# Root before the split of weight tile 1 at a branch's end, with that tile's low part on GpSimd, in a two-layer hybrid decoder step

## The reference

```python
xp = ffn_half_step(xp, g[0], g[1], ffn1_gate[l], ffn1_up[l], ffn1_down[l])
m_p, s_p = mix_prompt(rms_norm(xp, g[2]), lw)          # four head groups, input projection w_in, output w_out
xp = xp + rms_norm(m_p, g[3])
xp = ffn_half_step(xp, g[4], g[5], ffn2_gate[l], ffn2_up[l], ffn2_down[l])

def ffn_half_step(x, g_pre, g_post, w_gate, w_up, w_down):
    return x + 0.5 * rms_norm(swiglu(rms_norm(x, g_pre), w_gate, w_up, w_down), g_post)

def rms_norm(x, g):
    y = xf * lax.rsqrt(jnp.mean(xf * xf, axis=-1, keepdims=True) + NORM_EPS)
    return (y * g.astype(jnp.float32)).astype(x.dtype)
```

## Time and profile before

| | |
|---|---|
| median of 3 runs | 1602.6 us (1593.21, 1602.6, 1604.79) |
| the profiled execution's own time | 1603.99 us |
| its span in the profile | 1602.2 us |
| TensorE matmuls busy | 84% of the span |
| VectorE, ScalarE, GpSimd busy | 59%, 41%, 14% |
| mean granted TensorE clock | 0.87 of full |

### The profile page before, as it was taken

The page is one execution under the profiler, slowest core; times in us unless marked ns, Lnnn a source line. Parts: engine busy times, 40 slices in busy tenths (PEclk is TensorE's granted clock), DMA queues, the critical chain, the costliest instruction groups (busy, mean ns, idle before and its releaser), DMA issues.

```text
span 1602.2 us, 27946 instructions
## 1 busy us (share of the span) xinstructions
PE 1353.2 (84%) x9968; PEld 1257.8 (79%) x9968; DVE 944.8 (59%) x1508; ACT 652.6 (41%) x1054; POOL 216.7 (14%) x176
## 2 busy tenths in 40 slices
PE   6999979977587579999889999697866857699997
PEld 5999979966375369999889999697754735699996
DVE  4766355485654666664467654655756554666634
ACT  4655343343200255554456544434330004455543
POOL 1000010022332230000110000200323322200000
PEclk9999989967686589999989999899556966899998
DMA  6555554354461334555646556363444613255553
GB/s 213 183 184 160 163 177 131 96 155 138 147 192 49 93 105 134 184 172 162 182 129 190 172 155 181 106 199 97 129 130 138 185 38 106 83 184 183 159 168 94
DMA packets 286118, 234.15 MB, mean 146 GB/s; under 512 B 19898, under 2 KB 282018, under 8 KB 286056
## 3 DMA queue, kind: packets, MB, share of 16 engines
q1 hardware_dynamic: 286056, 233.37, 47.9%
HBM read 228.65 MB, written 5.37 MB: 146 GB/s over the span
## 4 chain that ended last, share of the span: by engine, by line
PE 76%; DVE 15%; ACT 3%; issue 3%; DMA 1%; SPq 0%; DVEq 0%; POOLq 0%; ACTq 0%
PE ps L1391 20%; PE ps L1392 19%; PE ps L1393 19%; PE ps L1590 2%; PE ps L1688 2%; DVE s L1114 2%; PE ps L1535 2%; DVE nlo L937 2%; PE ps L1687 1%; DVE yt L920 1%; PE ps L1538 1%; ACT whi L591 1%; PE ps L1504 1%; PE ps L1678 1%; PE ps L1733 1%
## 5 line engine op out<-in xcount | busy, mean ns | idle before, releaser
L1391 PE MATMUL ps<-nhi,whi 128*128 128x264 f32 x1936 | 564.2, 291 | 67.4 <-DVE nlo L937 47.0
L888 DVE TENSOR_TENSOR wlo<-raw,whi 128x1024 fp32r<-128x1024 f32 (+2 forms) x376 | 394.7, 1091 | 280.1 <-ACT whi L591 279.8
L1392 PE MATMUL ps<-nlo,whi 128*128 128x264 f32 x1936 | 558.5, 289 | 0.0
L1393 PE MATMUL ps<-nhi,wlo 128*128 128x264 f32 x1936 | 557.7, 288 | 0.0
L1391 PEld LDWEIGHTS ps<-nhi,whi 128*128 128x128 f32 x1936 | 375.2, 194 | 74.2 <-DVE nlo L937 35.9
L591 ACT ACTIVATE whi<-raw 128x1024 fp32r<-128x1024 f32 (+2 forms) x376 | 336.8, 945 | 190.9 <-PE ps L1393 113.4
L1392 PEld LDWEIGHTS ps<-nlo,whi 128*128 128x128 f32 x1936 | 375.4, 194 | 0.2
L1393 PEld LDWEIGHTS ps<-nhi,wlo 128*128 128x128 f32 x1936 | 373.2, 193 | 0.0
L1391 PE MATMUL ps<-hhi,whi 128*128 128x264 f32 x704 | 202.3, 287 | 9.1 <-DVE hlo L905 9.1
L1393 PE MATMUL ps<-hhi,wlo 128*128 128x264 f32 x704 | 201.4, 286 | 0.0
L1392 PE MATMUL ps<-hlo,whi 128*128 128x264 f32 x704 | 201.0, 286 | 0.0
(11 more groups left out here) (338 smaller groups left out, 1555.8 us busy)
## 6 DMA issues: line engine op xcount, KB each, us to landing
raw<-in_ffn_gate_dram SPq DMA_DIRECT2D x44, 1024.0 KB, 5.3
raw<-in_ffn_up_dram SPq DMA_DIRECT2D x44, 1024.0 KB, 5.4
raw<-in_ffn_down_dram SPq DMA_DIRECT2D x64, 704.0 KB, 4.5
raw<-in_w_in_dram SPq DMA_DIRECT2D x24, 1024.0 KB, 5.7
kslot<-in_cache_fox_k_dram SPq DMA_DIRECT2D x128, 128.0 KB, 2.7
vslot<-in_cache_fox_v_dram SPq DMA_DIRECT2D x128, 128.0 KB, 2.4
raw<-in_w_out_dram SPq DMA_DIRECT2D x8, 1024.0 KB, 5.1
kslot<-in_state_swa_k_dram SPq DMA_DIRECT2D x32, 128.0 KB, 2.7
```

The costliest lines, as they stand in the source:

```text
L888: tt2(wlo[s][:, a:b], raw[s][:, a:b], whi[s][:, a:b].bitcast(F32), ALU.subtract).then_inc(S(f"w_lo{s}"), 1)
L1391: mm(out, wh, hi_, start=first, stop=False)
L1392: mm(out, wh, lo_, start=False, stop=False)
L1393: return mm(out, wl, hi_, start=False, stop=last)
```

## The change

At five ends of a branch (dn1 to wi in both layers, wo to gu2 in both layers, dn2 to gu1 of layer 1):
- ScalarE no longer splits weight tile 1 of the next branch before the root. `pre` takes an argument `nxt`: it splits the first half of the tile before its loop, so right behind the root, and the second half inside the loop after tile 0 and before tile 1.
- VectorE no longer makes that tile's low part.
- GpSimd has a `lo` of its own. It makes the low part in two halves on its queue ahead of the sum of squares of the norm ahead of the next branch (e = 2, e = 4, and e = 0 of layer 1).

The first pair of layer 0 is as before.

```diff
-                    def hi(n, j, s, special=None, ahead=0):
+                    def hi(n, j, s, special=None, ahead=0, parts=(0, 1)):
...
-                        for a, b in HALVES[special or n]:
+                        for part in parts:
+                            a, b = HALVES[special or n][part]
                             act.activation(whi[s][:, a:b], raw[s][:, a:b], ACT.Copy).then_inc(S(f"w_hi{s}"), 1)
...
                             evac_y(n, e, j, 4 + m, 1, 0)
-                            if nxt[m]:
+                            if nxt[m] and nxt[m][0] == n:
                                 hi(*nxt[m], 1, ahead=ahead * m)
...
-                    def pre(e, ahead=0):
+                    def pre(e, ahead=0, nxt=None):
+                        if nxt:
+                            hi(nxt, 0, 1, ahead=ahead, parts=(0,))
                         for t in range(KT):
+                            if nxt and t == 1:
+                                hi(nxt, 0, 1, ahead=ahead, parts=(1,))
                             act.wait_ge(S("x_new"), V("x_new", 8 * (e // 2) + t + 1, ahead))
...
                     rms_of(1)
-                    pre(2)
+                    pre(2, nxt="wi")
...
-                            hi(*nxt, s)
+                            if s == 0 or j == 0:
+                                hi(*nxt, s)
                     rms_of(3)
-                    pre(4)
+                    pre(4, nxt="gu2")
...
-                        pre(0, ahead=1)
+                        pre(0, ahead=1, nxt="gu1")
...
+                    def lo(n, j, s):
+                        for i, (a, b) in enumerate(HALVES[n]):
+                            pool.wait_ge(S(f"w_hi{s}"), V(f"w_hi{s}", 2 * (P0[n] + j) + i + 1))
+                            tt_(wlo[s][:, a:b], raw[s][:, a:b], whi[s][:, a:b].bitcast(F32), ALU.subtract).then_inc(S(f"w_lo{s}"), 1)
+                    if l:
+                        lo("gu1", 0, 1)
                     for e in range(3):
+                        if e == 2:
+                            lo("wi", 0, 1)
                         sumsq(e)
...
                     for e in range(3, 6):
+                        if e == 4:
+                            lo("gu2", 0, 1)
                         sumsq(e)
...
                     lo("wi", 0, 0)
-                    lo("wi", 0, 1)
                     post(1)
...
-                    for s in range(2):
-                        lo("gu2", 0, s)
+                    lo("gu2", 0, 0)
                     post(3)
...
                     if l + 1 < DEPTH:
-                        for s in range(2):
-                            lo("gu1", 0, s, ahead=1)
+                        lo("gu1", 0, 0, ahead=1)
                     post(5)
```

## The result

The changed kernel takes 1606.7 us (median of 13 runs, 1603.6 to 1621.2) against 1598.9 us (median of 13 runs) for the kernel before. The ratio of the two is put at 1.0066, with a 95% interval of 1.0042 to 1.0089: about 10.6 us slower (the two medians by themselves lie 7.8 us apart). The prediction was 11.0 us more, a ratio of 1.0069, and 1613.6 us on the basis of the three times then known. The whole time moves by itself from execution to execution, so the five branch ends, where the change acts, are read first.

What follows compares the result with a forecast made beforehand. TensorE, busy 84% of the span, bounds the kernel; other engines' edits count only where it stands still. Stall of 17.2 us less 6.2 us of earlier roots gives +11.0 us on 1602.6, so 1613.6 us; range 1601 to 1622.

Steps and rivals of the forecast that it cites:

- The root comes earlier by 1.51 us at three ends: Ends at 580, 795 and 1372 us: without the split ahead, the root starts 0.04 us behind its matmul, gaining 1.51 us each.
- By 0.82 us at the two others: Ends at 225 and 1010 us: the mean-square matmul is late itself, so the root gains only 0.82 us each.
- A pass of GpSimd takes 2.35 us in this type: Each GpSimd low-part subtraction at the five ends takes 2.35 us, from the nearest form; bounds 1.90 and 3.21.
- The first yt is 1.27 us late, the second nlo ends at +9.21, nlo(3) at +13.27, the lateness is 3.4 us: Behind each root, GpSimd's passes and adds hold VectorE's instructions; stall 3.4 us per end, 17.2 us over five.
- The reciprocal does not exclude GpSimd: VectorE's reciprocal behind the root reads one tile and leaves GpSimd free; otherwise each end loses 0.84 us more, 1617.8 us.
- Everything behind the last nlo keeps its distance: Behind nlo(7) at each end, distances stay; the last add has 3.2 us to spare before TensorE asks for it.
- TensorE's pause of 9.4 us: TensorE's pause before the new branch was to be about 9.4 us in place of 8, costing nothing by itself.
- Net +11.0 us: Whole kernel: 17.2 us of stall less 6.2 us of earlier roots, 1613.6 us, 0.7% slower.
- Rival 1: At the five ends VectorE keeps going and GpSimd's passes stretch instead: -4.7 us, 1597.9 us; chance 0.11.
- rival 2: At the five ends GpSimd's pass is long, or the reciprocal excludes it: 1617.8 to 1622.2 us; chance 0.18.
- rival 3: At the five ends the root is not earlier, as load or root stay behind something else: +17.2, 1619.8 us; chance 0.05.
- The mishap that I gave 0.02: A mishap of the clock, such as a cold second weight tile at the lower clock; no size given, chance 0.02.

Runs made afterwards that it cites:

- Run 5: Changed kernel, but GpSimd makes only low half 0 and VectorE makes low half 1 behind its last nlo; ratio to the kernel before 0.9958, repeated 1.0012.
- run 1: Changed kernel, but the low part of weight tile 1 is back on VectorE, behind its last nlo; ratio to the kernel before 0.9993.
- run 3: Changed kernel, but GpSimd makes each half of the low part twice, one after the other; ratio to the kernel before 1.0186.
- run 2: Changed kernel, but ScalarE splits both halves of tile 1 ahead of the root again; low part stays on GpSimd; ratio to the kernel before 0.9968, repeated 0.9973.
- run 6: Changed kernel, but each GpSimd pass of 1024 columns is cut into two of 512; ratio to the kernel before 1.0059.
- run 4: Changed kernel, but ScalarE splits half 0 ahead of the root, half 1 behind it; both low halves on VectorE; ratio to the kernel before 0.998, repeated 0.9959.

## Why the prediction was right, step by step

- *The root comes earlier by 1.51 us at three ends*: 1.52 measured. The table load ran ahead of the wait for the matmul, as in the earlier trace rows (the 581.09 of the old matmul's end is from the earlier trace rows, not the earlier trace rows), and the 1.38 us of drain that the Trainium skill (ScalarE: Activation LUTs, "What ACT_TABLE_LOAD costs") adds did not show: 588.05 + 1.28 = 589.33, root at 589.72, 0.04 us behind the matmul's end.
- *By 0.82 us at the two others*: 0.83 at the first. At the second it was 1.36, as the mean-square matmul there took 0.71 us and not 1.25; it ran at the higher clock in both profiles of the changed kernel. GpSimd's last add took 1.35 us there all the same and TensorE stood 2.71 us ahead of it (2.63 before), so the reason that the prediction gives for the slow matmul, the long add, does not hold; what decides its clock stays open. Sum 6.8 us instead of 6.2.
- *A pass of GpSimd takes 2.35 us in this type*: 2.34, and 2.46 to 2.56 where it had to wait for VectorE.
- *The first yt is 1.27 us late, the second nlo ends at +9.21, nlo(3) at +13.27, the lateness is 3.4 us*: 1.29, +9.23, +13.2 (602.92 less 589.72), 3.36 to 3.46. Run 5 and run 1 show the terms apart, run 3 doubles them.
- *The reciprocal does not exclude GpSimd*: run 2 shows both at full speed for 1.80 us. The Trainium skill (SBUF — State Buffer, "Who interferes with whom") had it so, and its other half, that whoever issues first holds the other for a whole instruction, is what run 3 shows four times over.
- *Everything behind the last nlo keeps its distance*: at the ends it did, the second root came 4.5 us behind it in both kernels. TensorE's pause of 9.4 us: 9.33. Beyond the ends it did not: the rest of the span was 4.6 us longer in both profiles, 3 us of it by two more spells at the lower clock, which the prediction put at nothing; and the two stretches with the mixing stage were together 6.3 and 13.3 us shorter than in the kernel before.
- *Net +11.0 us*: 5 x 3.4 - 6.8 = 10.2 at the ends; the whole ran at +0.66% and +0.37% in two comparisons, 10.6 and 5.9 us of 1600. Only these ends were worked out, and there the mechanism and the size are right. That the whole came within 0.4 us of the 11.0 in the first comparison is partly luck: what moves outside the ends is as large as the effect, and the second comparison gave half of it.

Rival 1 (VectorE keeps going) is refuted by every hold above, rival 2 by the pass of 2.34 us, rival 3 by the root at 1.69 us. The mishap that I gave 0.02, a weight tile at the lower clock, did not come in the changed kernel's two profiles, but at three ends of runs 5 and 6.

What the change got wrong is then plain. At each end it took 2.4 us off VectorE while VectorE was waiting for the root anyway, and put 4.8 us onto GpSimd, the engine that excludes it, from 1.5 us after the root's start on, when TensorE and ScalarE wait for VectorE (from the first yt to the last nlo, some 13 us). The early root was worth 6.8 us, and run 4 keeps 4.5 of it.

## What to carry to other kernels

In this kernel, work moved from VectorE to GpSimd ran not beside VectorE but in place of it wherever VectorE ran instructions with two inputs in SBUF: count GpSimd's whole time outside the stretches in which VectorE idles or runs something with one input (here the reciprocal). Look at the place before the amount: the same ten passes cost some 16 us right behind the root and 0.6 us when they start two microseconds ahead of it. A race of this kind can also sit where nobody changed anything: in the mixing stage it costs 5.7 us or nothing, as VectorE comes a little behind or ahead of GpSimd. And when a change is worth 0.3% to 0.6%, sum the stretches that it touches from the profile; the whole time of one and the same kernel moved by up to 0.5% from one comparison to the next.

## What the runs showed that I had not expected

- The second weight tile's matmuls, without a gap, began at the lower of the two clock levels at two ends of run 6 and one of run 5, and ran at the higher at the other ends. The stretches of run 6 (columns as above):

```profile
247.30:252.50 5.20, 5.20 (x33) 5.20 (x32) 0.00 (x0) 0.00 (x0) 0.13 (x1) 0.67 0.00 0
607.60:611.00 3.40, 3.40 (x31) 3.40 (x29) 0.00 (x0) 0.00 (x0) 0.00 (x0) 1.00 0.00 0
```

  At the end at 228 us the clock had come back to full (1.00 from 242.0 to 246.0, while TensorE waited for VectorE tile by tile), was 0.50 from 247.3 to 250, and full again from 251 on. The tile's matmuls took 5.20 us in place of 3.40 (a few records are missing in the second row), and the second root came some 1.5 us later at each such end.
- The mixing stage, which the change leaves alone, holds the same race between VectorE and GpSimd as the branch's ends, and TensorE's clock decides who wins it (see above, where the rest moves).
- Run 2 is 0.3% faster than the kernel before in two comparisons, while its ends are 0.6 us slower. Its profiles show no lost race and few spells at the lower clock; why stays open.
